# A gather of token rows between the gate and the up products of an expert pair

## What is computed

```python
g_sel = jnp.argmax(g_logits, axis=-1)                      # one of 4 groups
e_p, e_i = lax.top_k(jax.nn.softmax(e_logits, axis=-1), 2)  # two of its 8 experts
...
def run(args):                                              # one block of one expert's tokens
    tok, wt, e = args
    xb = h_pad[tok]
    hid = jax.nn.silu(xb @ w_gate[e]) * (xb @ w_up[e])
    return (hid @ w_down[e]) * wt[:, None]
```

## Time and profile before

| | us |
|---|---|
| runs (3), median | 2255.46 |
| runs, lowest to highest | 2253.96 to 2256.44 |
| profiled execution, span from the first to the last instruction | 2248.1 |
| median less span, what lies around it | 7.4 |
| first mixture, first gate product of its loop to last up product | 309.7 to 825.2 |
| TensorE busy, share of the span | 95% |
| VectorE, ScalarE | 48%, 27% |
| DMA, mean over the span | 280 GB/s |

### The profile page before, as it was taken

The page is one execution under the profiler, slowest core; times in us unless marked ns, Lnnn a source line. Parts: engine busy times, 40 slices in busy tenths (PEclk is TensorE's granted clock), DMA queues, the critical chain, the costliest instruction groups (busy, mean ns, idle before and its releaser), DMA issues.

```text
span 2248.1 us, 32119 instructions
## 1 busy us (share of the span) xinstructions
PE 2137.4 (95%) x12440; PEld 1388.0 (62%) x12440; DVE 1087.9 (48%) x1969; ACT 613.4 (27%) x1214; POOL 12.7 (1%) x20
## 2 busy tenths in 40 slices
PE   7999999999999889889999999999999999999998
PEld 4744644444343347564444444478989989898997
DVE  5677541111111136642222222167888777787876
ACT  4446532112121114431111111133451012434001
POOL 0000000000000010000000000000000000000000
PEclk9999999999999999999999999999999999999999
DMA  8189169998999994229999999952345546235452
GB/s 349 76 360 427 75 253 378 386 383 352 429 392 429 428 386 184 113 91 384 427 429 429 428 429 428 427 243 104 140 170 187 187 153 255 110 114 206 181 190 98
DMA packets 50146, 629.97 MB, mean 280 GB/s; under 512 B 5888, under 2 KB 6912, under 8 KB 11904
## 3 DMA queue, kind: packets, MB, share of 16 engines
q1 hardware_dynamic: 45008, 611.30, 66.7%
q10 hardware_dynamic: 2880, 9.44, 1.0%
q0 software_dynamic: 2160, 7.87, 0.9%
HBM read 614.42 MB, written 14.16 MB: 280 GB/s over the span
## 4 chain that ended last, share of the span: by engine, by line
PE 71%; DMA 15%; DVE 10%; ACT 2%; issue 2%; SPq 1%; DVEq 0%; ACTq 0%
PE ps L1908 10%; DMA ring<-in_ex_gate 7%; PE ps L1847 7%; DMA ring<-in_ex_up 6%; PE ps L1376 6%; PE ps L1378 6%; PE ps L1377 6%; PE ps L1987 4%; PE ps L1989 4%; PE ps L1988 4%; PE ps L1924 3%; PE ps L1803 3%; PE ps L1881 2%; PE ps L1723 1%; PE ps L1399 1%
## 5 line engine op out<-in xcount | busy, mean ns | idle before, releaser
L1908 PE MATMUL ps<-ring,E 128*64 128x512 f32 x1152 | 260.1, 609 | 16.7 <-DMA ring<-in_ex_up 14.4
L1378 PE MATMUL ps<-hn_hi,w_lo 128*128 128x256 f32 x928 | 262.4, 283 | 0.0
L1847 PE MATMUL ps<-ring,E 128*64 128x512 f32 x992 | 221.1, 598 | 10.5 <-DMA ring<-in_ex_gate 7.5
L1908 PEld LDWEIGHTS ps<-ring,E 128*64 128x64 f32 x1152 | 87.9, 140 | 185.6 <-issue 185.6
L2736 DVE TENSOR_TENSOR E<-E,ps 128x512 f32<-128x512 f32 x18 | 12.4, 688 | 354.3 <-PE ps L1908 354.3
L1378 PEld LDWEIGHTS ps<-hn_hi,w_lo 128*128 128x128 f32 x928 | 177.8, 192 | 0.0
L1847 PEld LDWEIGHTS ps<-ring,E 128*64 128x64 f32 x992 | 73.8, 138 | 142.3 <-issue 142.1
L1102 ACT ACTIVATE hT<-ps 128x512 f32<-128x512 f32 x70 | 41.9, 599 | 370.1 <-PE ps L1803 370.1
L1376 PE MATMUL ps<-hn_hi,w_lo 128*128 128x256 f32 x480 | 138.3, 288 | 1.7 <-DVE w_lo L2838 1.7
L1377 PE MATMUL ps<-hn_lo,w_lo 128*128 128x256 f32 x480 | 135.7, 283 | 0.0
L2838 DVE TENSOR_TENSOR w_lo<-ring,w_hi 128x4096 fp32r<-128x4096 f32 x30 | 132.8, 4426 | 1.0
(11 more groups left out here) (557 smaller groups left out, 3847.0 us busy)
## 6 DMA issues: line engine op xcount, KB each, us to landing
ring<-in_ex_up SPq DMA_DIRECT2D x64, 2048.0 KB, 16.0
ring<-in_ex_gate SPq DMA_DIRECT2D x62, 2048.0 KB, 16.6
ring<-in_ex_down SPq DMA_DIRECT2D x60, 2048.0 KB, 14.8
ring<-in_w_layer SPq DMA_DIRECT2D x56, 2048.0 KB, 8.2
ring<-in_w_static SPq DMA_DIRECT2D x33, 2048.0 KB, 17.0
y_rows<-E ACTq DMA_DIRECT2D x36, 256.0 KB, 8.4
ring<-in_ex_down SPq DMA_DIRECT2D x8, 1024.0 KB, 16.2
E<-in_w_layer SPq DMA_DIRECT2D x2, 2048.0 KB, 13.0
```

Source lines behind the costliest of these rows:

```text
L1378: return pe.matmul(out, lo, xhi, start=False, stop=last)
L1847: ins = pe.matmul(ps[half(u), 2 + w, :], xg[:, k, half(u)], weights, start=k == 0, stop=k == KC - 1)
L1908: ins = pe.matmul(ps[half(u), 2 + w, :], xg[:, k, half(u)], slab(2 * w + u, (KC, DE))[:, k, :], start=k == 0, stop=k == KC - 1)
```

## The change

In the loop body of the first mixture the call of `gather(i + 2)` is moved from behind the loop over w into it, to the end of w = 0. The order becomes gate products, gather, up products, then the wait for `hid_ready`. Nothing else is edited.

```diff
                         ins.then_inc(sems["gu_mm"], 1)
-                    gather(i + 2)
+                        if w == 0:
+                            gather(i + 2)
                     pe.wait_ge(sems["hid_ready"], i + 1)
```

## The result

| | before | after |
|---|---|---|
| median of 6 runs each, us | 2254.71 | 2264.51 |
| lowest to highest, us | 2249.27 to 2256.44 | 2260.42 to 2268.19 |
| profiled execution, span, us | 2248.1 | 2266.5 |
| ratio of times, 95% interval | | 1.0048 [1.0035, 1.0061] |

The kernel became slower by 0.35 to 0.61%. Forecast were 0.25% and 2261.2 us; the sign was right, the measured median lies inside the range, and the loss is larger than its sum.

A forecast was written before the change was run, and what follows sets the result against it. TensorE was taken to bound ten pairs, the weight stream the later ones. 9.2 + 1.0 - 2.9 + 0.3 - 1.9 = 5.7 us, added to the median 2255.46, gave 2261.2 us; range 2256.8 to 2265.6.

The forecast's parts named there:

- The lost cover: Pairs that TensorE sets: without the gather behind the up products, TensorE waits for htmp; 1.15 us a pair taken.
- the break: Up products resuming behind other matmuls, here the gather, take 7.02 us instead of 6.87, 0.15 more a pair.
- The rival of a small break: Lost cover costs only 0.75 us a pair, transposes stay at 0.44; 2.2 us in all, 2257.7, no visible change; chance 0.27.
- The stretch of the first stalls: Around 580 to 620 us: 3.64 us stall and slow products vanish; following pair starts 7.3 us late, not 10.2.
- the first slip: Weight stream from the ninth pair: DMA queue runs dry before the late up loads; 0.7 to 1.1 us later, 1.0 taken.
- Its bytes fix the dates, and whether TensorE gathers or stands is nothing: Weight stream up to 815 us has no gap; the gather's 3.86 us there cost nothing and gain nothing.
- the gather fills the stalls: Rival: gather between load issue and wait shrinks 14.4 us of stalls and removes slow stretches; -11 us, 2244.5; chance 0.07.
- The second slip: Up slab issued at 643.9: asked for 3.9 us later, it lands 0 to 0.4 us late, 0.3 taken.
- loads follow each other without a break until the stall: Behind each late up load the weight stream was to run on without any further gap.
- 7.8 at least: Time from issue to landing of one weight slab with an empty DMA queue: 7.8 to 8.2 us.
- −1.9: Last pair: gate products slow at 9.8 us, up products at full rate, 7.05; the sum falls by 1.9 us.
- clearly slower: Rival: last up products also run at the slow rate, +7.5 us, 2263, or 2265.7 with another slow group; chance 0.18.

The follow-up runs named there:

- e_first8: New gather place in the first 8 pairs only, the old place behind them; 2260.37 us for 2256.22 of the kernel before, ratio 1.0020.
- e_later: Old gather place in the first 8 pairs, the new one in the 10 behind; ratio 0.9996 to the kernel before.
- e_silu: Changed kernel with htmp made as silu times silu, so VectorE no longer waits for the up products; ratio 0.9999 to the kernel before.
- e_double: Changed kernel with a second VectorE product, 0.69 us long, ahead of htmp; ratio 1.0079 to the kernel before.
- e_split: Changed kernel with 12 of the gather's 16 matmuls between gate and up products, 4 behind the up products; 2257.62 us for 2253.83, ratio 1.0018.
- r_after: The changed kernel measured and profiled again, no edit; 2261.31 us, ratio 1.0031 to the kernel before.
- r_before: The kernel before measured and profiled again, no edit; ratio 1.0010 to itself.
- e_warm: Kernel before with 16 more transposes in the last pair in front of the wait for up weights; ratio 1.0008 to the kernel before.
- e_silu_old: Kernel before with htmp made as silu times silu, the up result left out; ratio 1.0005 to the kernel before.
- e_double_old: Kernel before with a second VectorE product ahead of htmp; ratio 0.9997 to the kernel before.
- e_lateask: Kernel before with SP's free signal of the up slots held until the gather ends, up loads asked for 3.9 us later; ratio 1.0016.

## Why the prediction came out as it did

**The lost cover: right, within some hundredths.** Forecast was a pair of 27.1 us with 0.77 of standing, 0.23 of transposes and 0.15 of the break. The chain has 27.12, with 0.76 to 0.79, 0.22 and 0.17. At the ninth pair 9.1 us were lost for the 9.2 given. `e_first8` and `e_later` place the cost where TensorE sets the pace, `e_silu` and `e_double` tie it to htmp, `e_split` gives most of it back. The rival of a small break (0.75 us a pair) falls with the same row.

**The stretch of the first stalls: right in its sum.** The stall of 3.64 us at 580 and the slow products are gone, and the up products of that pair start at 593.30; taken from the stage's start that is 281.8, and the forecast 591.7 is 282.0. Their weights were in at 574.5 + 17.5 = 592.0, and the next pair's at 601.6 + 21.4 = 623.0, that is 280.5 and 311.5 from the stage's start for the 280.5 and 310.8 forecast, so the first slip (1.0 taken) was right for the first and 0.7 us too small for the second. The thirteenth pair starts 8.5 us late in the profiled pair of executions, 7.4 by the mean of `r_after` and after (328.35) against the mean of the five traces in the old order (before, `r_before`, `e_warm`, `e_silu_old`, `e_double_old`: 321.0); forecast 7.3. The way there differed. The waits did not stay with the up products; TensorE stands in front of gate and down weights:

```profile
612.17 7.09 PE L1908 MATMUL ps<-ring,E 128*64 128x512 f32 x32 [2.45 <-DMA ring<-in_ex_gate]
...
806.01 7.09 PE L1925 MATMUL ps<-ring,E 128*64 128x512 f32 x32 [0.39 <-DMA ring<-in_ex_down]
815.80 7.09 PE L1937 MATMUL ps<-ring,E 128*64 128x512 f32 x32 [2.70 <-DMA ring<-in_ex_gate]
...
826.79 7.09 PE L1937 MATMUL ps<-ring,E 128*64 128x512 f32 x32 [1.64 <-DMA ring<-in_ex_up]
```

With the gather's 3.9 us ahead of the up products TensorE comes to the up weights after they have landed, but comes to the next gate weights before. The chain goes from one down load to the next:

```profile
722.55 22.21 DMA ring<-in_ex_down
...
783.66 22.22 DMA ring<-in_ex_down
```

Three stand in a row here, 30.56 us from one to the next. "Its bytes fix the dates, and whether TensorE gathers or stands is nothing" is what these and `e_later` show. The rival "the gather fills the stalls" did happen and brought nothing. The Trainium skill's page "DMA: Bandwidth & Descriptors" (Rules for kernel authors) advises to issue loads early, compute, and wait late; here more compute stood ahead of the up wait, the wait vanished (14.4 us in the loop), and others nearly as long appeared (10.5 and 1.6 us), with DMA share at 1.01 before and after.

**The second slip: mis-sized.** The term that failed is "by 0 to 0.4 us (0.3 taken)". From the thirteenth pair to the last up products the traces with the old order take 184.9 to 185.8 us (six, the five above and `e_first8`, mean 185.3) and those with the new order, or only the late signal, 186.3 to 188.1 (seven, mean 187.1). The slip is 1.8 us, not 0.3 (1.2 between the profiled executions of before and after alone). `e_lateask` shows that the late signal alone can do it (187.3).

The forecast took the slip as the time to landing with an empty queue less what the trace had, for the first of the two loads. For that load it was right: counted from the start of the thirteenth pair (629.56 in before, 639.83 in after) it landed at 26.0 in before and at 26.3 in after. What failed is the sentence behind it, that from there "loads follow each other without a break until the stall". The pair's down loads come next; they were issued at 656.1 in before and 667.5 in after, and landed after (before, then after; of the two of after only one landing is in the trace):

```profile
DMA to landing us min/median/max: 10.1/12.4/14.6
```
```profile
DMA to landing us min/median/max: 10.9/10.9/10.9
```

From the thirteenth pair's start the first is in at 36.6 and 38.5, so what was 0.3 us late is now 1.9 (1.3 between `r_before` and `r_after`). A window of before, and the one of after that lies 10 us later as its pair does, columns as in the earlier trace rows:

```profile
640.00:650.00 10.00, 10.00 (x54) 5.65 (x51) 2.82 (x9) 2.22 (x3) 0.00 (x0) 1.00 1.01 410
```
```profile
650.00:660.00 10.00, 9.21 (x48) 3.81 (x46) 1.42 (x3) 0.60 (x1) 0.00 (x0) 1.00 1.00 387
```

In the first 40 us from the pair's start before moved 15.8 MB and after 15.3 (windows 629.6 to 670 and 639.8 to 680), a difference worth about 1 us at 428 GB/s. In `e_lateask` it is the up load itself that lands late, at 28.2. Where in the stream the time goes, and whether the down loads, which after asks for 1.1 us later because its pairs are longer, have a part in it, was not tested apart.

The prediction also gave 6.8 us for a slab by the Trainium skill's page "DMA: Bandwidth & Descriptors" (Anatomy of one DMA). That section's fit is for transfers that GpSimd issues, and these are SP's. No gate or up load of the stage landed sooner than 7.5 us after its issue in any trace; in before the shortest, issued at 324.3, took 7.6, so "7.8 at least" was a little high.

**The last pair: the step "−1.9" failed.** It has two parts. "So the gate takes 9.8 us" was wrong: the standing was 2.70 us and not 4, in part because the down products had waited too (0.39), and the gate products took 7.09 (8.60 in `r_after`). The up products did run at the full rate (7.09), as forecast, but "what follows the stage is one chain and moves along" was wrong: with the up products shorter, the gathered rows of `y_rows` are late instead. TensorE of after waits for them where before did not (L1430, 2.25 us); `r_after` has 1.91 and `e_warm`, on the old kernel, 1.97. In after more follows: the last eight down products, behind this wait, took 3.42 us where before, `r_after` and `e_warm` have 1.94, with PEclk at 0.56 from 846.0 to 849.6.

```profile
846.10 3.42 PE L1964 MATMUL ps<-ring,E 128*64 128x512 f32 x8
```

The slow rate had moved from the up products to the end of the stage. From the start of the last up products to the product behind the stage, after took 29.0 and `r_after` 27.2 us, before and `r_before` 28.0 and 28.1. On average nothing was gained, and over all thirteen traces this stretch runs from 26.8 to 30.9 us.

**The sum as measured**, means of the two traces of each kernel: 9.1 at the ninth pair, +7.6 at the thirteenth, +9.2 at the last up products and +9.2 behind the stage (543.4 less 534.2), where 9.2, 7.3, 7.6 (for the last up weights; 8.5 for their products, which were to wait for the small matmuls) and 5.7 were forecast. Of the 3.5 us missed, 1.9 are the gain in the last pair that did not come and 1.6 the weights' delay, mostly the second slip. The medians say +9.8 us in the first measurement, +5.1 in the second; 9.2 lies inside the intervals of both ratios (7.9 to 13.8 us, and 4.3 to 9.7).

The rival "clearly slower" gave the right size (+7.5 to +10.2 us) for the wrong reason: it put the slow rate on the last up products, and they ran at the full rate in both profiles of after. The slow rate did fall on the path elsewhere, on the last eight down products of after, 1.5 us of its stage, and not in `r_after`, where the stage lost 8.3 us (542.5 for 534.2) without it.

## What to carry to other kernels

Before a block is moved, ask what ran beside it on the other engines: here sixteen matmuls hid one VectorE step, and each pair in the engine-bound stretch paid 1.15 us for their move. In the stretch that the full weight stream sets here, placing work in front of a wait moved the wait to the next load and gained nothing, whereas lost cover there cost next to nothing either, so the place of such a block should be judged by the stretches that the engine sets. A gain at the end of a stage counts only up to the next thing that becomes late; look for it in the trace before it is booked.

## What the runs showed of the hardware that was not expected

- 32 products of 64 weight columns take 6.87 us behind others of their kind and 7.02 behind matmuls of 128 columns, and a gather in two parts between them takes 0.20 us more than in one (`e_split`). That the number of columns is the reason was not tested.
- A transpose group that follows the wait for htmp stands in the chain with 0.66 us, behind uninterrupted matmuls with 0.44.
- In after, waits of 2.45 to 2.70 us were followed by products at full rate, 7.09 us. In before, after 3.64 and 4.08 us the products took 9.68 and 9.92. In `r_after` two groups of gate products, each after such a wait of 2.7 us, took 8.46 and 8.60 us and three others, after 1.94 to 2.62 us, 7.09; the last up products started at 515.3 us as in after, so that rate lay beside the stream, as forecast for the gate. And 1.84 us behind small matmuls sufficed for 9.82 in before, whereas 1.64 us in the same place of after did not (7.09, timeline above). `e_warm`, with more transposes and no wait in that place, had 7.09 too. What decides was not settled.
- The last eight down products, behind the wait for the gathered rows, took 2.86 to 3.68 us in the five traces in which that wait was 2.25 to 3.30 us (after, `e_silu_old`, `e_split`, `e_double`, `e_lateask`), and 1.94 in the eight with 1.97 us or less.
- The DMA share stood at 1.00 with 387 GB/s moved (after, 650 to 660 us) and at 1.01 with 429 (694 to 827): a share of 1 is not yet the full rate.
